# Three of sixteen gate stages kept in on-chip memory, and eight gather slots placed behind the dense part

## What is computed

```
v1, i1 = top_k(sc[:, :, 0], 16);  v2, i2 = top_k(sc[:, :, 1], 16)      # two key tables of 128
top_sc, pos = top_k(v1[:, None] + v2[None, :], 16);  eidx = 128 * i1 + i2 at pos
gate = softmax(top_sc)
hid  = gelu(einsum('td,thkd->thk', x, u_tab[eidx]))
out  = einsum('thk,thkd->td', gate * hid, v_tab[eidx])
```

## Time and profile before

| | us |
|---|---|
| median of three runs | 1824.52 |
| range of the three | 1823.31 to 1825.52 |
| the profiled execution | 1828.5 |
| span of its trace | 1826.7 |
| TensorE busy | 1693.6 (93%) |
| VectorE busy | 1225.8 (67%) |
| GpSimd busy | 688.4 (38%) |
| ScalarE busy | 368.1 (20%) |

### The profile page before, as it was taken

The page is one execution under the profiler, slowest core; times in us unless marked ns, Lnnn a source line. Parts: engine busy times, 40 slices in busy tenths (PEclk is TensorE's granted clock), DMA queues, the critical chain, the costliest instruction groups (busy, mean ns, idle before and its releaser), DMA issues. The chain is left out here.

```text
span 1826.7 us, 19835 instructions
## 1 busy us (share of the span) xinstructions
PE 1693.6 (93%) x7088; PEld 1257.6 (69%) x7088; DVE 1225.8 (67%) x2439; ACT 368.1 (20%) x910; POOL 688.4 (38%) x598
## 2 busy tenths in 40 slices
PE   7998999999777988898897999999999999999998
PEld 6887888878555776787785666666666666666633
DVE  2352111899688868898986999776656666666676
ACT  1141123111330344642660001101000000000101
POOL 0000000234034438631665555555444544544542
PEclk9999999999778999899888999999999999999999
DMA  6523434779246949995999999999999999999997
GB/s 192 176 93 115 162 116 153 256 251 346 77 138 198 378 166 372 339 329 183 358 343 414 409 409 410 409 407 409 410 409 410 398 410 409 398 410 396 389 409 273
DMA packets 238300, 563.09 MB, mean 308 GB/s; under 512 B 17068, under 2 KB 125276, under 8 KB 236156
## 3 DMA queue, kind: packets, MB, share of 16 engines
q0 software_dynamic: 82944, 302.03, 42.9%
q1 hardware_dynamic: 122180, 243.02, 36.3%
q10 hardware_dynamic: 33080, 16.79, 3.1%
HBM read 539.46 MB, written 21.66 MB: 307 GB/s over the span
## 5 line engine op out<-in xcount | busy, mean ns | idle before, releaser
L796 POOL DMA_INDIRECT M<-in_u_tab,IDX x288 | 324.5, 1127 | 731.3 <-DVE PEER L1763 359.6
L803 POOL DMA_INDIRECT M<-in_v_tab,IDX x288 | 360.2, 1251 | 379.7 <-DVE X L1784 307.7
L1107 PE MATMUL PSB<-XN,M 128*128 128x256 f32 x2048 | 469.2, 384 | 8.7 <-DMA M<-in_u_blocks 4.2
L1115 PE MATMUL PSB<-M,HST 128*128 128x512 f32 x1024 | 461.0, 596 | 13.3 <-DVE HST L1840 12.6
L1107 PEld LDWEIGHTS PSB<-XN,M 128*128 128x128 f32 x2048 | 393.5, 193 | 109.4 <-issue 52.5
L1763 DVE CUSTOM_DVE_ANT_0 M<-M,XN 128x1024 f32<-128x1024 f32 x288 | 351.9, 1223 | 144.0 <-DMA M<-in_u_tab,IDX 142.7
L1784 DVE SCALAR_TENSOR_TENSOR X<-M,PEER,X 128x1024 f32<-128x1024 f32 x256 | 328.0, 1281 | 102.8 <-DMA M<-in_v_tab,IDX 99.7
L1115 PEld LDWEIGHTS PSB<-M,HST 128*128 128x128 f32 x1024 | 194.6, 191 | 217.9 <-issue 202.2
L845 PE MATMUL PSB<-M 128*128 128x256 f32 (+1 forms) x1408 | 333.3, 398 | 9.1 <-DVE M L1412 7.8
L845 PEld LDWEIGHTS PSB<-M 128*128 128x128 f32 x1408 | 269.9, 193 | 65.4 <-DVE M L1412 8.7
L852 PE MATMUL PSB<-M 128*128 128x256 f32 (+1 forms) x1056 | 249.5, 397 | 3.8 <-DMA M<-in_w_out 1.6
(11 more groups left out here) (217 smaller groups left out, 1074.6 us busy)
## 6 DMA issues: line engine op xcount, KB each, us to landing
M<-in_u_blocks SPq DMA_DIRECT2D x128, 512.0 KB, 6.9
M<-in_v_tab SPq DMA_DIRECT2D x128, 512.0 KB, 6.8
M<-in_w_in SPq DMA_DIRECT2D x24, 1024.0 KB, 6.2
M<-in_w_pq SPq DMA_DIRECT2D x16, 1024.0 KB, 8.2
gate_spill<-M ACTq DMA_DIRECT2D x16, 1024.0 KB, 13.5
M<-gate_spill SPq DMA_DIRECT2D x16, 1024.0 KB, 10.7
M<-in_w_out SPq DMA_DIRECT2D x8, 1024.0 KB, 4.9
M<-in_w_mq SPq DMA_DIRECT2D x8, 1024.0 KB, 8.0
```

What stands on the lines that cost most here:

```text
L796: pool.indirect_dma_start(out=UA[:, s % RR, :], out_offset=None, in_=utab, in_offset=bass.IndirectOffsetOnAxis(ap=IDX[:, n:n + 1], axis=0) ...
L803: pool.indirect_dma_start(out=VA[:, s % RR, :], out_offset=None, in_=vtab, in_offset=bass.IndirectOffsetOnAxis(ap=IDX[:, n:n + 1], axis=0) ...
L1107: last = pe.matmul(PSB[:, 4 + b % 2, 0:2 * P], UBLK[:, b % SR, c, :], XN[:, 1:3, c * P:(c + 1) * P], start=(c == 0), stop=(c == DC - 1))
L1115: last = pe.matmul(PSB[:, 2 * t + hf, :], WR[:, b % WRING, t * P:(t + 1) * P], VBLK[:, b % SR, hf * 512:(hf + 1) * 512], start=(b == 0), s ...
```

## The change

Three things are done.

1. The last three stages (48 of the tokens of tile 2) are no longer written to DRAM and read back. `KEPT` = 3 staging buffers hold them to the end, in memory that is free by then (`LAST`). The 13 others (`NSP`) are written and read as before, in groups of 13/16 of the size. The ring `HR` and the buffers `GR` for the groups that are read back move to other addresses.
2. `w(b)` becomes two multiplications, one over the 208 columns of the 13 stages and one over the 48 columns of the kept ones. Its counter counts two for each block. SyncE issues the first three group reads after `lk` 16 instead of after `lk` 20, and waits there for the last `gb` and the 13 writes.
3. `mid` and `last` become the middle of steps 4 and 6 instead of the starts of steps 5 and 7: eight gather slots (a `d` and a `v` each) fewer stand in the dense part, as many as before among the leading `lk`, and eight more among the block pairs.

```
-STAGED_IN = [c % 2 for c in range(NCH // 2)] + [c % 3 for c in range(NCH // 2)]
+KEPT = 3
+NSP = NCH - KEPT
+STAGED_IN = [(c + 1) % 2 for c in range(NCH // 2)] + [(c + 1) % KEPT for c in range(NCH // 2)]
...
-    one, early, mid, last = step(1), step(3), step(EARLY_STEPS), step(EARLY_STEPS + G0_STEPS)
+    half = lambda i: slots.index(("d", i, TOPK // 2))
+    one, early, mid, last = step(1), step(3), half(EARLY_STEPS - 1), half(EARLY_STEPS + G0_STEPS - 1)
...
-        STG = [cut(M, SCO + r * P * CH_TOK, P, CH_TOK) for r in range(2)] + [ar(12488, P, CH_TOK)]
+        STG = [cut(M, SCO + r * P * CH_TOK, P, CH_TOK) for r in range(KEPT)]
+        LAST = cut(M, SCO, KEPT, P, CH_TOK)
-        HR = ar(0, HRING, 2 * P)
-        GR = [ar(off, NCH, GRP, CH_TOK) for off in (12488, 6656, 8704)]
+        HR = ar(2048, HRING, 2 * P)
+        GR = [ar(8192 + k * NSP * GRP * CH_TOK, NSP, GRP, CH_TOK) for k in range(GRING)]
...
-                if seg == ("lk", HRING - 4):
+                if seg == ("lk", HRING - 8):
                     sp.wait_ge(relaid_s, 64)
-                    for r in range(3):
-                        sp.wait_ge(gs_out[r], 16 * STAGED_IN.count(r))
+                    sp.wait_ge(oh_used, len(SMALL))
+                    for r in range(KEPT):
+                        sp.wait_ge(gs_out[r], 16 * STAGED_IN[:NSP].count(r))
                     for k in range(GRING):
                         gate_group(k)
...
-                pe.wait_ge(wr_done, b + 1)
+                pe.wait_ge(wr_done, 2 * (b + 1))
...
-                if at + OH_TOK == CH_TOK:
+                if at + OH_TOK == CH_TOK and c < NSP:
...
-                runs = lambda x: x.rearrange("p (c x) -> p c x", c=NCH)
-                dve.tensor_tensor(runs(WR[:, b % WRING, :]), runs(HR[:, b % HRING, :]), GR[k % GRING][:, :, b % GRP, :], ALU.mult).then_inc(wr_done, 1)
+                if b == 0:
+                    dve.wait_ge(g_out, len(SMALL))
+                wr, hr, far = WR[:, b % WRING, :], HR[:, b % HRING, :], NSP * CH_TOK
+                runs = lambda x: x.rearrange("p (c x) -> p c x", x=CH_TOK)
+                dve.tensor_tensor(runs(wr[:, 0:far]), runs(hr[:, 0:far]), GR[k % GRING][:, :, b % GRP, :], ALU.mult).then_inc(wr_done, 1)
+                dve.tensor_tensor(runs(wr[:, far:]), runs(hr[:, far:]), LAST[:, :, b, :], ALU.mult).then_inc(wr_done, 1)
```

More of the change, by code:

```diff
@@ L633, in load_block @@
             sp.dma_start(WB[:, i % NW], a[name][0, :, col:col + BW].rearrange("(c p) n -> p c n", p=P)).then_inc(w_in[i % NW], 16)
-        spill = nc.dram_tensor("gate_spill", (NBLK // GRP, P, NCH, GRP * CH_TOK), F32, kind="Internal").ap()
+        spill = nc.dram_tensor("gate_spill", (NBLK // GRP, P, NSP, GRP * CH_TOK), F32, kind="Internal").ap()
         block = ctx.enter_context(nc.Block())
@@ L710, in gate_group @@
                 if k >= GRING:
-                    sp.wait_ge(wr_done, GRP * (k - GRING + 1))
+                    sp.wait_ge(wr_done, 2 * GRP * (k - GRING + 1))
                 sp.dma_start(GR[k % GRING].rearrange("p c i x -> p c (i x)"), spill[k]).then_inc(gr_in[k % GRING], 16)
@@ L1322, in lk @@
                 if b >= HRING:
-                    act.wait_ge(wr_done, b - HRING + 1)
+                    act.wait_ge(wr_done, 2 * (b - HRING + 1))
                 act.activation(HR[:, b % HRING, :], PSB[:, 4 + b % 2, 0:2 * P], ACT.Gelu).then_inc(h_done, 1)
@@ L1342, in gb @@
                     if r == 2 and STAGED_IN.index(2) == c:
-                        wait_job(act, ("pq", 1, 15))
+                        wait_job(act, ("sc", NP, 3))
                     else:
```

## The result

The changed kernel takes 1837.73 us (median of 7 runs, 1834.14 to 1846.37), the kernel before 1824.52 (7 runs beside it, 1820.92 to 1829.8). The ratio is 1.0076, 95% interval 1.0054 to 1.0097: **0.8% slower, about 13 us**. The forecast was 1827.5, that is +3 us, and no difference that can be told was its likeliest outcome. The time lies 0.3 us inside the stated range, at its slow end; the direction of the +3 was right, but the loss is some 13 us and clear of noise. The profiled execution took 1842.43 us, its span is 1840.4 us, against 1828.5 and 1826.7 before: 13.7 us more in the two traces.

The account below looks back on a forecast made before the run. The prediction took the gather stream, held by full DMA engines, to bound the kernel. Its terms, -2.5 (dense part), -1 (wait at first `w`) and +6.7 (blocks, including writes), gave +3.2, forecast as +3 us, 1827.5; range 1813 to 1838.

Parts of the forecast that it names:

- What bounds the kernel: Block pairs: the gather stream, held by the DMA engines, is the slower; VectorE loses 0.25 us a block to TensorE.
- The reads, -8.1, and the gathers, +21.9: Blocks: 3.15 MB less to read at 2.56 us a MB, against 16 more gathers at 1.37 us each.
- The split of `w`, 0: Blocks: two products cost VectorE 0.16 us more a block, 20 us in all, covered by its 34% idle time.
- The writes, -6.9: After 955, where DMA sets the pace: two of the three dropped stage writes count as won, ends 0 to -10.4.
- The stated other end, +12.6: Whole kernel: slow end of the sum, -0.9 + 0 + 13.5, with none of the three dropped writes counted.
- The moved slots among the leading `lk`, 0: From 847 to 955: the same one-hot rows and slots stand as before, so no change in time.
- The dense part, -2.5: Attention output products grow 0.5 to 4.5 us, the last projection shrinks 5.4; sum -0.9 to -4.9, taken as -2.5.
- The wait at the first `w`, -1: Start of the blocks: the 2.90 us wait for the last gate writes goes; -1 us counted, 0 to -2.9.
- The lead: VectorE's lead over TensorE in the blocks: lost at 0.42 instead of 0.25 us a block, gone near block 65, not 84.
- The signs to look for: Trace marks set beforehand: projection start and end, first `w` about 993, leads at blocks 20 and 70, TensorE and DMA shares.
- Rival A: End of the kernel: TensorE sets it after all, starting blocks earlier; about -10 us, 1814.5; chance 0.22.
- Rival B: Blocks after the lead is gone: stalls cost double through TensorE's lower clock; +13 us, 1837.5; chance 0.16.

Follow-up runs that it names:

- e2: The kernel before with only the eight gather slots moved from the dense part to the block pairs, nothing kept: 1848.23 us, ratio 1.0128.
- e1: The changed kernel with the gather slots where they were before the change (kept stages, no moved slots): 1814.45 us, ratio 0.9934 to the kernel before.
- e3: The kernel before with the gate product split in two (208 and 48 columns), all 16 stages still going through DRAM: 1827.36 us, ratio 1.0015.
- e10: The changed kernel with the last three stages also written to DRAM and never read: 1838.88 us, ratio 1.0070 to the kernel before.
- e5: Kept stages without the change's slot moves, but four more gather slots in the dense part and four fewer in the blocks: 1814.84 us, 0.9931 to the kernel before.
- e11: The changed kernel with the last three stages written to DRAM and written again to another place, never read: 1864.54 us, 1.0204 to the kernel before.

## Why the forecast was wrong, step by step

- **What bounds the kernel: right.** The gather stream, held by full DMA engines, was the late one. e2 and e1 show it from both sides.
- **The reads, -8.1, and the gathers, +21.9: right as a sum.** Over 1.02 they give +13.5; from w(0) on the trace shows +12.7. Each for itself is off by about 3 us, in opposite directions: e2 has +18.8 there for the gathers alone, e1 -10.7 for the reads alone.
- **The split of `w`, 0: right**, by e3.
- **The writes, -6.9: the step that failed most.** It took two of three writes into the full stretch; the trace has one there (1.05 MB). And it took every MB that goes as time won in the end, because the share read 1.04; the freed room stayed half unused. e10, which brings the three writes back, changes the whole time by -1 us, give or take 4. It does show a gain of 5.6 us up to the first `w`, most of which the blocks behind take back. The stated other end, +12.6 with none of the writes counted, is near what was measured.
- **The moved slots among the leading `lk`, 0: failed.** The number of slots there stayed the same, so nothing was booked. e2 shows +4.2 us in this stretch. Net, it took 0.2 us more than before where the forecast had -7.9.
- **The dense part, -2.5: probably failed.** The last projection gave its -5.4 to the tenth. The stretch ahead of it grew by 5.0 instead of the 2.9 that the value taken rests on, and 0.9 more before the projection starts: +0.5 in all. TensorE's waits for ScalarE's scaled copies of the one-hot rows (L1337) rose from 5.6 to 9.5 us there. Since traces of one program differ by some 4 us here, -2.5 is not excluded.
- **The wait at the first `w`, -1: failed.** The wait went, w(0) did not come earlier.
- **The lead.** By the prediction's own rows, 5.4 us at block 80 and 0.25 us a block, it would last to about block 102 and not 84. TensorE waits from about block 81 on all the same, because ScalarE's small gelu makes it wait before the lead of `w` is gone.
- With 0 for the writes, the dense part and the wait the sum is +13.5 and the forecast 1838.0; the measured median is 1837.7. That it fits so well is in part luck: the terms of the blocks and of the leading `lk` have errors of 3 to 6 us that cancel.
- **The signs to look for.** Seen: no wait for `gate_spill`; TensorE's share 98% (460.54 of 470) from 1110 on; the DMA share above 1. Missed: the last projection starts 6.2 us later, not up to 4, and ends 0.8 later, not 2 to 3 sooner; w(0) at 998.75, not 993; the lead of block 20 at 9.7 us, not 16 to 22; the lead gone by block 40, not 65, and at 5.9 in block 70.
- **Rival A** fell with the same two credits. It is true of e1, where TensorE does set the end. **Rival B** gave 1837.5, nearly the measured time. Part of its mechanism is in the trace: from the start of `vd(0)` to the end the changed kernel takes 839.8 us and e5, with hardly a stall, 811.2; of the 28.6 between them some 20 are waits of TensorE (the 9.0, 1.5 and 9.6 of its two products after 1010) and about 9 are products at a lower clock. But these 9 are no price on top. The DMA engines are full all the while (1.02), and the bytes alone account for the time. That TensorE would have waited in these 9 us at full clock is argued from this, not shown by a run. The equal number does not make B the cause.

**The best version.** e1, the kept stages without the moved slots, takes 1814.45 us: 0.7% under the kernel before and 1.4% under the changed one.

## What to carry to other kernels

Credit a removed transfer only if the stream that is late has its next request ready when the room comes free. A share of 1.04 in a short stretch at a boundary does not show that; a long stretch in which the lead shrinks does, and there bytes times price was right to 1 us for what came and went together (to 3 us for each alone). Where a change both wins and pays, check each win by itself: this one paid its price in the stretch that was read well, and had its gains booked in two that were not. Where two resources lie as close as here (TensorE some 12 us from the DMA engines), a gain is capped by the other, while a loss is paid. Ask of every engine what stands ahead, in its program order, of the work that others wait for: here a small gelu passed VectorE's lateness on to TensorE. And know how well a stretch repeats before reading a difference in it: one here repeats to 0.1 us, the one before it to 4.

## What the runs showed of the hardware

- A 1 MB write of 512-byte pieces was issued in 0.37 us in the kernel before and in e10, one about every 11 us. In e11, with six such writes inside 48 us, one held ScalarE for 20.43 us, and everything behind it in ScalarE's program.
- A V product of eight passes is 3.60 us after TensorE has worked for 16 us and 6.09 us after it idled 10.73; in the changed kernel the idle time lies 16 us ahead of it, and the products behind that pay: 64 passes in 16.52 us, where 16 passes at full clock take 3.62.
- Two VectorE multiplications over 208 and 48 columns take 370 and 201 ns, one over 256 takes 420. The Trainium skill, "VectorE: DVE Perf Modes", section on the errata, gives (N + 151) / 0.96 ns for float32, which would be 374 and 207; the trace agrees to 3%.
